# One transformer layer with product-key experts, fp32 split in two halves: order of the first expert table's products and place of the wait on its low half

## The chip, the cores and the metric

One core of a Trainium2 chip. The metric is the device time of one execution in microseconds (us). Before the change three runs took 958.69, 960.25 and 960.53 us, median 960.25.

## What is computed

One decoder layer on 256 tokens of width 1024: RMS norm, one input projection, eight heads of softmax attention and eight of stick-breaking attention, an output projection, then a feed-forward part of 16384 single-neuron experts chosen by product keys, then a gated per-layer embedding. The change is in the experts. The reference, cut to them:

```
# x: (256, 1024) normalised; u_table, v_table: (16384, 1024)
e_idx, gates = ...            # per token 8 heads x 16 experts, by two top-16 searches and a softmax
u = u_table[idx_c]
hid = gelu(einsum('cd,ced->ce', x_c, u))
out = einsum('ce,ced->cd', g_c * hid, v_table[idx_c])
```

The kernel does not gather. It multiplies all tokens with all 16384 rows of `u_table`, applies GELU, multiplies by a dense matrix of gates (zero for experts that were not chosen), and multiplies that with all of `v_table`.

## The kernel before

**Precision.** Every large product is made of three. A float32 operand is split into a high half (ACT casts it to the TensorE format `fp32r`) and a low half (the operand minus its high half, again `fp32r`), and hi x hi, hi x lo and lo x hi are summed in PSUM. The helper `three` (L1233) issues them in this order, piece by piece of the contraction.

**The first table's stage.** `u_table` comes as 128 tables `u_chunks[n]` of 128 experts: a tile of 128 x 1024 floats, 512 KB. One table is one *step* (numbered 0 to 127 here). The ring has four places (`RING`), q = n mod 4:

- SP loads table n into `t_raw[:, q]` once step n - 4 is done (`hid_done`, L361 to L364). After the last table the same ring goes on with `v_chunks` (L365 to L367).
- ACT makes `t_hi[:, q]` (`table_hi`, L597 to L599; semaphore `t_hi_ready`), two tables ahead of the GELU that it does between them (`LEAD` = 2).
- POOL makes `t_lo[:, q]` in the place of `t_raw` (`table_lo`, L1206 to L1209; semaphore `t_lo_pool`), after `t_hi_ready`.
- PE makes the step's 24 products (`hidden`, L1487 to L1490): eight pieces c of the contraction, for each `t_hi` x `xt_hi`, `t_hi` x `xt_lo`, `t_lo` x `xt_hi`, 128 x 128 weights with 256 columns (tokens), all into one PSUM bank. They are recorded under the helper's lines: L1236, L1237, L1238. The last one increments `hid_done`.
- ACT takes the bank through GELU, into `slots` for the first 40 tables (`FIRST`), in place for the later ones; there DVE multiplies it into `slots` (`late_gelu`, L1089).

**What PE waits for.** `u_lo(q, i)` (L271) is the semaphore `t_lo_pool` and the number of the table, and PE waits for it at the head of each step. There are three places: the first four steps (L1492 to L1498), the loop `u_steps` for steps 4 to 35 and again 36 to 39 (L1503 to L1508; the picks are transposed in between, L1510 to L1520), and `late_step` for steps 40 to 127 (L1530 to L1542). Each has one more wait at the head, for the PSUM bank or, in the first three, for the key scores (`s_out`, `gelu_done` or `late_used`). A late step has its 24 products followed, in three of four steps, by two waits and the four matmuls of `gates` (L1523 to L1528), until 64 sets are done. The order on every engine is the order written; the loops of all engines meet only through semaphores.

```
def u_lo(q, i):
    return t_lo_pool, RING * i + q + 1
```

**After the stage** PE takes the second table (`expert_sum`, L1553, lines L1565, L1567, L1568, 512 columns each), with the low halves made by DVE (L943), and then the gated embedding.

Of the kernel before, what the change touches and what calls it, by code (L numbers as in the profile page):

```python
# [27 lines left out]
P = 128  # L28
SEQ = 256
D = 1024  # L30
DC = D // P
# [13 lines left out]
RING = 4  # L45
LEAD = 2
FIRST = 40
# [24 lines left out]
def layer_program(nc, x, x_t, p_t, rel_bias, bucket_onehot, consts, qk_gain, w_in, w_out, w_query,  # L72
# [5 lines left out]
    with ctx:  # L78
# [11 lines left out]
        def tile(name, shape, offset, dt=f32):  # L90
            return nc.alloc_sbuf_tensor_at(name, shape, dt, offset=offset)

        h = tile("h", [P, TT, D], where["h"])
        xt_hi = tile("xt_hi", [P, DC, SEQ], where["xt_hi"], f32r)
        xt_lo = tile("xt_lo", [P, DC, SEQ], where["xt_lo"], f32r)
# [69 lines left out]
        t_lo = tile("t_lo", [P, RING, D], ZONE, f32r)  # L165
# [5 lines left out]
        t_hi = tile("t_hi", [P, RING, D], ZONE + 4 * 7168, f32r)  # L171
# [18 lines left out]
        def xt_half(k, c):  # L190
            return half(c // 2 + (4 if k == 2 else 0), c % 2)
# [4 lines left out]
        def hid_bank(q):  # L196
            return bank[(4, 5, 6, 5)[q % RING]][:, 0:SEQ]
# [12 lines left out]
        def sem(name):  # L210
            return ctx.enter_context(nc.semaphore(name))
# [36 lines left out]
        t_hi_ready, t_lo_ready, t_lo_pool = sem("t_hi_ready"), sem("t_lo_ready"), sem("t_lo_pool")  # L248
        lanes_ready, ones_ready, late_used = sem("lanes_ready"), sem("ones_ready"), sem("late_used")
        table_row = sem("table_row")  # L250
        hid_done, gelu_done = sem("hid_done"), sem("gelu_done")
# [19 lines left out]
        def u_lo(q, i):  # L271
            return t_lo_pool, RING * i + q + 1
# [120 lines left out]
        def _(act):  # L393
# [23 lines left out]
            def root(k, first, last):  # L417
                _, ms, rstd = norm_stats(k)
                nc.scalar.activation(rstd[:, first:last], ms[:, first:last], ACT.Sqrt).then_inc(root_ready, 1)
# [799 lines left out]
        def _(pe):  # L1219
            mm = nc.tensor.matmul  # L1220

            def transpose(src, tt, c, dst):
                return nc.tensor.transpose(dst, src[:, tt, P * c:P * (c + 1)], ident)
# [9 lines left out]
            def three(dst, pairs, last=None):  # L1233
                n = len(pairs)
                for c, ((ah, al), (bh, bl)) in enumerate(pairs):
                    mm(dst, ah, bh, start=(c == 0), stop=False)  # L1236
                    mm(dst, ah, bl, start=False, stop=False)  # L1237
                    ins = mm(dst, al, bh, start=False, stop=(c == n - 1))  # L1238
                return ins
# [40 lines left out]
            for c in range(DC):  # L1280
                pe.wait_ge(xt_lo_ready, c + 1)
                pe.wait_ge(quarter_lo, c + 1)
                for tt in range(TT):
                    t, dst = slice(P * tt, P * (tt + 1)), bank[4 + tt][:, :]
                    mm(dst, xt_hi[:, c, t], w_hi[:, 0, c, :], start=(c == 0), stop=False)
                    mm(dst, xt_hi[:, c, t], w_lo[:, 0, c, :], start=False, stop=False)
                    ins = mm(dst, xt_lo[:, c, t], w_hi[:, 0, c, :], start=False, stop=(c == DC - 1))
# [7 lines left out]
            for tt in range(TT):  # L1295
                ins = mm(bank[1][:, P * tt:P * (tt + 1)], neg_ones, diag[:, P * tt:P * (tt + 1)], start=True, stop=True)
# [8 lines left out]
            for g in range(8):  # L1305
                for tt in range(TT):
                    ins = nc.tensor.transpose(bank[g // 2][:, 256 * (g % 2) + P * tt:256 * (g % 2) + P * (tt + 1)],
                                              qk_nat[:, tt, 2 * g:2 * g + 2, :].rearrange("p a b -> p (a b)"), ident)
# [8 lines left out]
            for i in range(4):  # L1317
                if i >= 2:
                    pe.wait_ge(columns_out, 2 + i)
                for e in range(2):  # L1320
                    r = slice(HD * e, HD * (e + 1))
                    mm(bank[3 * e + i // 2][:, 256 * (i % 2):256 * (i % 2) + 256], qkt_s[r, 4 + i, 0:P], qkt_s[r, i, :],
                       start=(i % 2 == 0), stop=True, skip_group_check=True)
                for e in range(2):
                    r = slice(HD * e, HD * (e + 1))
                    ins = mm(bank[3 * e + 2][:, P * i:P * (i + 1)], qkt_s[r, 4 + i, P:SEQ], qkt_s[r, i, P:SEQ],
                             start=(i == 0), stop=True, skip_group_check=True)
# [42 lines left out]
            for hh in range(NH):  # L1370
                if hh % 4 == 0:
                    pe.wait_ge(s_exp, 1 + hh // 4)
                ins = nc.tensor.transpose(bank[hh // 4][:, P * (hh % 4):P * (hh % 4 + 1)], s0[:, hh, :], ident)
# [5 lines left out]
            for tt in range(TT):  # L1379
                for hh in range(NH):  # L1380
                    e, i = hh % 2, hh // 2
                    cols = slice(512 + HD * hh, 512 + HD * (hh + 1))
                    dst = bank[6 + tt][:, HD * hh:HD * (hh + 1)]
                    c = 256 * i + P * tt
                    ins = mm(dst, sb_w[:, e, c:c + P], v_all[:, 0, cols], start=True, stop=(tt == 0))
                    if tt:
                        ins = mm(dst, sb_w[:, e, 1024 + P * i:1024 + P * (i + 1)], v_all[:, 1, cols], start=False,
                                 stop=True)
# [3 lines left out]
            for hh in range(NH):  # L1392
                ins = mm(bank[0][:, HD * hh:HD * (hh + 1)], probs_t[:, hh // 4, P * (hh % 4):P * (hh % 4 + 1)],
                         v_all[:, 0, HD * hh:HD * (hh + 1)], start=True, stop=True)
# [3 lines left out]
            for hh in range(NH):  # L1398
                if hh % 4 == 0:
                    pe.wait_ge(s_exp, 3 + hh // 4)  # L1400
                for ss in range(2):
                    c = 256 * (hh % 2) + P * ss
                    ins = nc.tensor.transpose(bank[2 + hh // 2][:, c:c + P], s1[:, hh, P * ss:P * (ss + 1)], ident)
# [10 lines left out]
            for hh in range(NH):  # L1414
# [5 lines left out]
                for ss in range(2):  # L1420
                    c = 256 * (hh % 2) + P * ss
                    ins = mm(bank[1][:, HD * hh:HD * (hh + 1)], probs_t[:, place, c:c + P],
                             v_all[:, ss, HD * hh:HD * (hh + 1)], start=(ss == 0), stop=(ss == 1))
# [31 lines left out]
            for tt in range(TT):  # L1455
                pe.wait_ge(xs_ready, tt + 1)
                for c in range(DC):
                    ins = transpose(xs, tt, c, xt_half(2, c)[:, P * tt:P * (tt + 1)])
# [25 lines left out]
                    key_scores(n - 1)  # L1484
            key_scores(3)

            def hidden(q):  # L1487
                three(hid_bank(q), [((t_hi[:, q, P * c:P * (c + 1)], t_lo[:, q, P * c:P * (c + 1)]),
                                               (xt_hi[:, c, :], xt_lo[:, c, :])) for c in range(DC)]
                      ).then_inc(hid_done, 1)  # L1490

            for q in range(RING):  # L1492
                pe.wait_ge(*u_lo(q, 0))
                if q == RING - 1:
                    pe.wait_ge(gelu_done, q - 1)
                else:
                    pe.wait_ge(s_out, q + 1)
                hidden(q)  # L1498

            def bank_before(q):  # L1500
                return 2 if q % 2 else RING

            def u_steps(first, last):  # L1503
                with pe.Fori(first // RING, last // RING) as i:
                    for q in range(RING):
                        pe.wait_ge(*u_lo(q, i))
                        pe.wait_ge(gelu_done, RING * i + q - bank_before(q) + 1)
                        hidden(q)  # L1508

            u_steps(RING, PICKS_AT)  # L1510
            pe.wait_ge(hit_used, 2 * TT)
            for q in range(2):
                for tt in range(TT):
                    ins = nc.tensor.transpose(bank[q][:, P * tt:P * (tt + 1)], pick[:, tt, q, :], ident)
                ins.then_inc(pick_t_done, 1)
            pe.wait_ge(picks_ready, 1)
            for tt in range(TT):
                ins = nc.tensor.transpose(bank[2][:, P * tt:P * (tt + 1)],
                                          gate[:, tt, :, :].rearrange("p a b -> p (a b)"), ident)
            ins.then_inc(pick_t_done, 1)  # L1520
            u_steps(PICKS_AT, FIRST)

            def gates(k, s):  # L1523
                pe.wait_ge(hots_ready, s + 1)
                for q in range(4):
                    ins = mm(pairs[k][:, q, :, :].rearrange("p a b -> p (a b)"), hot_i[:, k, q, :],  # L1526
                             hot_j[:, k, q, :, :].rearrange("p a b -> p (a b)"), start=True, stop=True)
                ins.then_inc(gates_done, 1)  # L1528

            def late_step(q, j, first=False, last=False):  # L1530
                m, s = PAIR * j + q, 6 * j + 3 * (q // RING) + q % RING
                k = (3 * (q // RING) + q % RING) % 2
                pe.wait_ge(*u_lo(q, 2 * j + FIRST // RING))
                if first and q < bank_before(q):
                    pe.wait_ge(gelu_done, m + FIRST - bank_before(q) + 1)
                else:
                    pe.wait_ge(late_used, m - bank_before(q) + 1)
                hidden(q % RING)
                if q % RING < 3 and not (last and s >= SETS):
                    if not (first and s < 2):  # L1540
                        pe.wait_ge(gated, s - 1)
                    gates(k, s)  # L1542

            for q in range(PAIR):
                late_step(q, 0, first=True)
            with pe.Fori(1, N_PAIRS - 1) as j:
                for q in range(PAIR):
                    late_step(q, j)
            for q in range(PAIR):
                late_step(q, N_PAIRS - 1, last=True)  # L1550
# [39 lines left out]
            for q in range(RING - 2, RING):  # L1590
                ins = expert_sum(q, N_KEYS // RING - 1, tiles=(0,))
# [6 lines left out]
            for u, (tt, d0, width, b) in enumerate(END_PARTS):  # L1598
                t, d = slice(P * tt, P * (tt + 1)), slice(d0, d0 + width)
                dst = bank[b][:, 0:width]  # L1600
# [4 lines left out]
                for c in range(DC):  # L1605
                    if c % 2 == 0:
# [3 lines left out]
                    ins = mm(dst, xt_lo[:, c, t], wg_hi[:, c, d], start=False, stop=(c == DC - 1),  # L1610
                             skip_group_check=True)
# [66 lines left out]
```

## Time and profile before

| | |
|---|---|
| runs | 958.69, 960.25, 960.53 us |
| the profiled execution | 959.54 us, of which the span of the trace is 957.8 |
| granted clock of TensorE over the first table's stage | 1.00 of full speed |
| first table's stage, 188 to 580 us | PE busy 391.8 us, DVE 337.0, ACT 305.9, POOL 305.2 |
| loads of the first table | 128 of 512 KB, median 3.3 us from issue to landing |
| second table's stage | from 580.6 us on |

How to read it: PE is the matmul unit, PEld its weight loads, DVE the vector engine, ACT the scalar engine, POOL the GpSimd engine, SP the engine that issues the loads. A matmul is drawn longer than it holds the array, since matmuls overlap, so "busy" says that something is in flight; distances between starts tell the pace. L12 is line 12 of the kernel.

### The profile page before, as it was taken

Reading aid. Unit: us, or ns where it says so; the run is one execution under the profiler, and the core shown is the slowest. Engines: PE = TensorE matmul, PEld = TensorE weight load, DVE = VectorE, ACT = ScalarE, POOL = GpSimd, SP = SyncE. Lnnn points to the kernel's source line nnn. Section 1 sums busy time; section 2 is a strip of 40 time slices with the busy share of each in tenths; the row PEclk is TensorE's granted clock in tenths of the full one; section 3 lists DMA queues with packets and bytes.
Section 4 is the critical chain, followed back from the end, with each engine's and each line's share of the span. In section 5 each row is a group of like instructions: output and inputs, shape, how many; then the busy total and the mean of one; then the engine's idle time right before and its main releaser. Section 6 shows DMA issues by size and latency. Waiting matters only on the chain.

```text
span 957.8 us, 19183 instructions
## 1 busy us (share of the span) xinstructions
PE 948.6 (99%) x6222; PEld 863.8 (90%) x6222; DVE 686.2 (72%) x1391; ACT 614.4 (64%) x1037; POOL 329.9 (34%) x147
## 2 busy tenths in 40 slices
PE   8999999999999999999999999999999999999998
PEld 6887889999999999999999998788888888888887
DVE  6748863999975888888888874655555555566763
ACT  7568664456676888888888874555445445555643
POOL 0002310288888777777777772000000000000000
PEclk9999999999999999999999999999999999999999
DMA  9770363055565454444445455555566666555531
GB/s 332 272 289 1 113 255 133 2 178 192 179 189 183 158 175 157 171 157 172 164 165 168 160 176 181 193 193 185 193 238 242 236 230 234 197 196 188 191 105 44
DMA packets 46459, 172.08 MB, mean 180 GB/s; under 512 B 5043, under 2 KB 8540, under 8 KB 44892
## 3 DMA queue, kind: packets, MB, share of 16 engines
q1 hardware_dynamic: 46284, 171.40, 52.4%
q8 instruction: 19, 0.31, 0.1%
q10 hardware_dynamic: 144, 0.28, 0.1%
q14 instruction: 12, 0.10, 0.0%
HBM read 169.55 MB, written 2.11 MB: 179 GB/s over the span
## 4 chain that ended last, share of the span: by engine, by line
PE 89%; DVE 5%; DMA 3%; issue 2%; ACT 1%; POOL 1%; SPq 0%; DVEq 0%; POOLq 0%; ACTq 0%
PE bank L1237 12%; PE bank L1236 12%; PE bank L1238 12%; PE pair L1565 12%; PE pair L1567 12%; PE pair L1568 12%; PE pair L1526 3%; DMA w_raw<-w_in 2%; PE pair L1270 1%; PE pair L1272 1%; PE pair L1271 1%; PE bank L1610 1%; PE bank L1609 1%; PE bank L1252 1%; PE bank L1253 1%
## 5 line engine op out<-in xcount | busy, mean ns | idle before, releaser
L599 ACT ACTIVATE t_hi<-t_raw 128x1024 fp32r<-128x1024 f32 x256 | 270.5, 1057 | 187.3 <-DMA t_raw<-v_chunks 162.5
L1208 POOL TENSOR_TENSOR t_lo<-t_raw,t_hi 128x1024 fp32r<-128x1024 f32 x130 | 312.1, 2409 | 146.8 <-ACT t_hi L599 146.8
L1237 PE MATMUL bank<-xt_lo,t_hi 128*128 128x256 f32 x1024 | 287.4, 281 | 0.0
L1236 PE MATMUL bank<-xt_hi,t_hi 128*128 128x256 f32 x1024 | 287.2, 280 | 0.2 <-POOL t_lo L1208 0.2
L1238 PE MATMUL bank<-xt_hi,t_lo 128*128 128x256 f32 x1024 | 286.6, 280 | 0.0
L943 DVE TENSOR_TENSOR t_lo<-t_raw,t_hi 128x1024 fp32r<-128x1024 f32 x126 | 154.4, 1225 | 137.3 <-ACT t_hi L599 137.1
L1565 PE MATMUL pair<-t_hi,g_hi 128*128 128x512 f32 x512 | 199.6, 390 | 0.4 <-DVE g_lo L1123 0.4
L1567 PE MATMUL pair<-t_lo,g_hi 128*128 128x512 f32 x512 | 199.3, 389 | 0.0
L1568 PE MATMUL pair<-t_hi,g_lo 128*128 128x512 f32 x512 | 199.3, 389 | 0.0
L1236 PEld LDWEIGHTS bank<-xt_hi,t_hi 128*128 128x128 f32 x1024 | 192.8, 188 | 0.4 <-POOL t_lo L1208 0.4
L1238 PEld LDWEIGHTS bank<-xt_hi,t_lo 128*128 128x128 f32 x1024 | 193.1, 189 | 0.0
L1237 PEld LDWEIGHTS bank<-xt_lo,t_hi 128*128 128x128 f32 x1024 | 192.5, 188 | 0.0
L1565 PEld LDWEIGHTS pair<-t_hi,g_hi 128*128 128x128 f32 x512 | 96.1, 188 | 21.3 <-DVE g_lo L1123 1.3
L1567 PEld LDWEIGHTS pair<-t_lo,g_hi 128*128 128x128 f32 x512 | 96.1, 188 | 19.9
L1568 PEld LDWEIGHTS pair<-t_hi,g_lo 128*128 128x128 f32 x512 | 96.1, 188 | 19.7
L1076 DVE TENSOR_SCALAR hot_j<-bank,pick_t 128x128 fp32r<-128x128 f32 x256 | 86.9, 401 | 0.0
L650 ACT ACTIVATE hot_j<-hot_j,ratio 128x128 fp32r<-128x128 f32 x256 | 82.0, 394 | 0.0
L1092 DVE TENSOR_TENSOR slots<-slots,bank 128x256 f32 (+1 forms) x88 | 36.2, 412 | 31.4 <-ACT bank L663 31.4
L663 ACT ACTIVATE bank<-bank 128x256 f32<-128x256 f32 x88 | 32.4, 368 | 39.3 <-PE bank L1238 32.4
L1123 DVE TENSOR_TENSOR g_lo<-slots,g_hi 128x256 fp32r<-128x256 f32 x128 | 53.7, 420 | 0.6 <-ACT g_hi L673 0.6
L673 ACT ACTIVATE g_hi<-slots 128x256 fp32r (+1 forms) x128 | 51.2, 400 | 0.6 <-DVE slots L1092 0.6
L1086 DVE TENSOR_TENSOR slots<-slots,pair 128x512 f32 (+1 forms) x64 | 44.0, 687 | 7.5
(281 smaller groups left out, 1283.2 us busy)
## 6 DMA issues: line engine op xcount, KB each, us to landing
t_raw<-u_chunks SPq DMA_DIRECT2D x128, 512.0 KB, 3.3
t_raw<-v_chunks SPq DMA_DIRECT2D x128, 512.0 KB, 3.2
w_raw<-w_query SPq DMA_DIRECT2D x4, 2048.0 KB, 8.0
w_raw<-w_in SPq DMA_DIRECT2D x3, 2048.0 KB, 10.6
w_raw<-w_out SPq DMA_DIRECT2D x2, 2048.0 KB, 8.4
wg_raw<-w_gate SPq DMA_DIRECT2D x8, 512.0 KB, 4.8
w_raw<-w_in SPq DMA_DIRECT2D x7, 512.0 KB, 9.4
w_raw<-w_in SPq DMA_DIRECT2D x2, 1024.0 KB, 10.5
```

The costliest lines, as they stand in the source:

```text
L599: nc.scalar.activation(t_hi[:, q % RING, :], t_raw[:, q % RING, :], ACT.Copy).then_inc(t_hi_ready, 1)
L650: ins = nc.scalar.activation(hot_j[:, k, q, 1, :], hot_j[:, k, q, 0, :].bitcast(f32), ACT.Copy, scale=ratio[:, bass.ds(4 * s + q, 1)])
L943: nc.vector.tensor_tensor(t_lo[:, q % RING, :], t_raw[:, q % RING, :], t_hi[:, q % RING, :].bitcast(f32), ALU.subtract).then_inc(t_lo_read ...
L1076: nc.vector.tensor_scalar(hot_j[:, k, q, 0, :], lanes, pick_t[:, 1, bass.ds(t, 1)], pick_t[:, 2, bass.ds(t, 1)], ALU.is_equal, ALU.mult).t ...
L1123: nc.vector.tensor_tensor(g_lo[:, k, :], src, g_hi[:, k, :].bitcast(f32), ALU.subtract).then_inc(g_lo_ready, 1)
L1208: nc.gpsimd.tensor_tensor(t_lo[:, q, :], t_raw[:, q, :], t_hi[:, q, :].bitcast(f32), ALU.subtract).then_inc(t_lo_pool, 1)
L1236: mm(dst, ah, bh, start=(c == 0), stop=False)
L1237: mm(dst, ah, bl, start=False, stop=False)
L1238: ins = mm(dst, al, bh, start=False, stop=(c == n - 1))
L1565: mm(dst, g_hi[:, q, t], t_hi[:, q, d], start=first and q == 0, stop=False, skip_group_check=True)
L1567: mm(dst, g_hi[:, q, t], t_lo[:, q, d], start=False, stop=False, skip_group_check=True)
L1568: ins = mm(dst, g_lo[:, q, t], t_hi[:, q, d], start=False, stop=True, skip_group_check=True)
```

## The change

Of the 24 products of a step, the sixteen with the high half of the table are issued first, for all eight pieces, and then the eight with the low half. At the head of a step PE waits for `t_hi_ready` of that table instead of `t_lo_pool`; the wait for `t_lo_pool` stands between the sixteenth and the seventeenth product. All three places are changed in the same way. The other waits, the other engines and the other stages stay.

```diff
--- before.py
+++ after.py
@@ -1484,18 +1484,24 @@
                     key_scores(n - 1)
             key_scores(3)
 
-            def hidden(q):
-                three(hid_bank(q), [((t_hi[:, q, P * c:P * (c + 1)], t_lo[:, q, P * c:P * (c + 1)]),
-                                               (xt_hi[:, c, :], xt_lo[:, c, :])) for c in range(DC)]
-                      ).then_inc(hid_done, 1)
+            def hidden(q, lo_ready):
+                dst = hid_bank(q)
+                for c in range(DC):
+                    t = slice(P * c, P * (c + 1))
+                    mm(dst, t_hi[:, q, t], xt_hi[:, c, :], start=(c == 0), stop=False)
+                    mm(dst, t_hi[:, q, t], xt_lo[:, c, :], start=False, stop=False)
+                pe.wait_ge(*lo_ready)
+                for c in range(DC):
+                    ins = mm(dst, t_lo[:, q, P * c:P * (c + 1)], xt_hi[:, c, :], start=False, stop=(c == DC - 1))
+                ins.then_inc(hid_done, 1)
 
             for q in range(RING):
-                pe.wait_ge(*u_lo(q, 0))
+                pe.wait_ge(t_hi_ready, q + 1)
                 if q == RING - 1:
                     pe.wait_ge(gelu_done, q - 1)
                 else:
                     pe.wait_ge(s_out, q + 1)
-                hidden(q)
+                hidden(q, u_lo(q, 0))
 
             def bank_before(q):
                 return 2 if q % 2 else RING
@@ -1503,9 +1509,9 @@
             def u_steps(first, last):
                 with pe.Fori(first // RING, last // RING) as i:
                     for q in range(RING):
-                        pe.wait_ge(*u_lo(q, i))
+                        pe.wait_ge(t_hi_ready, RING * i + q + 1)
                         pe.wait_ge(gelu_done, RING * i + q - bank_before(q) + 1)
-                        hidden(q)
+                        hidden(q, u_lo(q, i))
 
             u_steps(RING, PICKS_AT)
             pe.wait_ge(hit_used, 2 * TT)
@@ -1530,12 +1536,12 @@
             def late_step(q, j, first=False, last=False):
                 m, s = PAIR * j + q, 6 * j + 3 * (q // RING) + q % RING
                 k = (3 * (q // RING) + q % RING) % 2
-                pe.wait_ge(*u_lo(q, 2 * j + FIRST // RING))
+                pe.wait_ge(t_hi_ready, RING * (2 * j + FIRST // RING) + q + 1)
                 if first and q < bank_before(q):
                     pe.wait_ge(gelu_done, m + FIRST - bank_before(q) + 1)
                 else:
                     pe.wait_ge(late_used, m - bank_before(q) + 1)
-                hidden(q % RING)
+                hidden(q % RING, u_lo(q, 2 * j + FIRST // RING))
                 if q % RING < 3 and not (last and s >= SETS):
                     if not (first and s < 2):
                         pe.wait_ge(gated, s - 1)
```

## Rows read from the trace of the kernel before

**Rows 1.** The page: span, engines, the chain that ended last.
```profile
span 957.8 us, 19183 instructions
...
PE 948.6 (99%) x6222; PEld 863.8 (90%) x6222; DVE 686.2 (72%) x1391; ACT 614.4 (64%) x1037; POOL 329.9 (34%) x147
...
PE 89%; DVE 5%; DMA 3%; issue 2%; ACT 1%; POOL 1%; SPq 0%; DVEq 0%; POOLq 0%; ACTq 0%
```

**Rows 2.** PE's waits: who waited for whom, us in total, times, longest.
```profile
PE pair L1565 <- DVE g_lo L1123: 0.4, 1, 0.4
...
PE bank L1236 <- POOL t_lo L1208: 0.2, 1, 0.2
```

**Rows 3.** Costliest groups: count | busy us, mean ns | idle before.
```profile
L1208 POOL TENSOR_TENSOR t_lo<-t_raw,t_hi 128x1024 fp32r<-128x1024 f32 x130 | 312.1, 2409 | 146.8 <-ACT t_hi L599 146.8
L1237 PE MATMUL bank<-xt_lo,t_hi 128*128 128x256 f32 x1024 | 287.4, 281 | 0.0
L1236 PE MATMUL bank<-xt_hi,t_hi 128*128 128x256 f32 x1024 | 287.2, 280 | 0.2 <-POOL t_lo L1208 0.2
L1238 PE MATMUL bank<-xt_hi,t_lo 128*128 128x256 f32 x1024 | 286.6, 280 | 0.0
```

**Rows 4.** Timeline around the head of step 2: start us, length us, instruction.
```profile
190.59 1.06 ACT L599 ACTIVATE t_hi<-t_raw 128x1024 fp32r<-128x1024 f32 x1
...
191.73 2.40 POOL L1208 TENSOR_TENSOR t_lo<-t_raw,t_hi 128x1024 fp32r<-128x1024 f32 x1 [11.69 <-ACT t_hi L599]
...
193.74 0.28 PE L1238 MATMUL bank<-xt_hi,t_lo 128*128 128x256 f32 x1
...
194.19 0.39 PE L1236 MATMUL bank<-xt_hi,t_hi 128*128 128x256 f32 x1 [0.17 <-POOL t_lo L1208]
...
194.41 0.28 PE L1237 MATMUL bank<-xt_lo,t_hi 128*128 128x256 f32 x1
```

**Rows 5.** Timeline around the head of step 24.
```profile
252.67 1.06 ACT L599 ACTIVATE t_hi<-t_raw 128x1024 fp32r<-128x1024 f32 x1 [0.19 <-DMA t_raw<-u_chunks]
...
253.80 2.49 POOL L1208 TENSOR_TENSOR t_lo<-t_raw,t_hi 128x1024 fp32r<-128x1024 f32 x1 [0.39 <-ACT t_hi L599]
...
256.34 0.28 PE L1238 MATMUL bank<-xt_hi,t_lo 128*128 128x256 f32 x1
256.46 0.35 PE L1236 MATMUL bank<-xt_hi,t_hi 128*128 128x256 f32 x1
256.64 0.28 PE L1237 MATMUL bank<-xt_lo,t_hi 128*128 128x256 f32 x1
```

**Rows 6.** Timeline: heads of steps 4, 19, 71, 72 and 80, gates and POOL before 72.
```profile
199.95 0.28 PE L1236 MATMUL bank<-xt_hi,t_hi 128*128 128x256 f32 x1
...
242.34 0.28 PE L1236 MATMUL bank<-xt_hi,t_hi 128*128 128x256 f32 x1
...
400.58 0.63 PE L1526 MATMUL pair<-hot_j,hot_i 128*128 128x256 f32 x4
...
400.73 2.41 POOL L1208 TENSOR_TENSOR t_lo<-t_raw,t_hi 128x1024 fp32r<-128x1024 f32 x1 [0.88 <-ACT t_hi L599]
...
401.05 0.28 PE L1236 MATMUL bank<-xt_hi,t_hi 128*128 128x256 f32 x1
...
403.86 0.28 PE L1236 MATMUL bank<-xt_hi,t_hi 128*128 128x256 f32 x1
...
429.25 0.28 PE L1236 MATMUL bank<-xt_hi,t_hi 128*128 128x256 f32 x1
```

**Rows 7.** Timeline of the query projection: every second to fourth column block's first product.
```profile
144.50 0.28 PE L1270 MATMUL pair<-xt_hi,w_hi 128*128 128x256 f32 x1
...
155.81 0.28 PE L1270 MATMUL pair<-xt_hi,w_hi 128*128 128x256 f32 x1
...
176.22 0.28 PE L1270 MATMUL pair<-xt_hi,w_hi 128*128 128x256 f32 x1
...
181.82 0.28 PE L1270 MATMUL pair<-xt_hi,w_hi 128*128 128x256 f32 x1
```

## The prediction

> **What bounds the kernel now.** I read the page first. TensorE is busy 948.6 us of a span of 957.8 us, and the chain that ended last is 89% PE [rows 1]. So the question is only how much the change gives to, or takes from, the uninterrupted row of matmuls. The changed lines run in the stage of the first expert table. It goes from the first product of step 0 at about 188 us to the last one of step 127 at about 580 us: 128 steps of 24 products, and between them 64 sets of four gate matmuls and six transposes.
>
> Second view: PE's waits [rows 2]. The wait on `t_lo`, which the change moves behind sixteen products, is listed once, with 0.2 us. Nothing else in this stage is listed.
>
> That view can hide small losses, because a matmul is drawn 280 ns long [rows 3] while the next one starts about 117 ns later. So I went by start times. A step of 24 products takes 2.82 to 2.83 us from start to start: fifteen steps from 199.95 to 242.34 give 42.39 / 15 = 2.826 us, 117.7 ns a product [rows 6]. I compared each start in the stage with the one before. A loss shows at step 2, and in smaller size at steps 20, 24 and 28 (each the head of a loop iteration); at all other step heads the interval is the usual 0.11 to 0.12 us, apart from the resumption after the transposes (step 36) and the first step, which the change leaves as they are.
>
> **Step 2** [rows 4]. POOL begins `t_lo` of table 2 at 191.73 and takes 2.40 us, until 194.13. The last product of step 1 starts at 193.74, the first of step 2 at 194.19: 0.45 us where 0.12 is usual. The next one follows after 0.22 instead of 0.12, a restart from an empty queue. Together 0.33 + 0.10 = 0.43 us. `t_hi` of the table was ready at 190.59 + 1.06 = 191.65, over 2 us before.
>
> **Step 24** [rows 5]. `t_lo` is ready at 253.80 + 2.49 = 256.29, the step starts at 256.46 on time, but its second product comes 0.18 us later, 0.06 more than usual. So the table was released just 0.17 us ahead and PE's queue was almost empty. This pattern stands three times in all; I put 0.2 us for the three together. The other steps of the early loop have a similar, thin lead of POOL (its 2.4 us [rows 3] against a step of 2.8), but lose nothing. `t_hi` was ready at 252.67 + 1.06 = 253.73, a lead of 2.7 us. In the loop of the late steps POOL leads by more: 400.73 + 2.41 = 403.14 against a start at 403.86 [rows 6].
>
> **The change, part by part.**
> Removed from the head of each step: the wait on `t_lo`, replaced by one on `t_hi`. It gives back what step 2 and the three thin steps lose: -0.43 - 0.2 = -0.6 us. All later work of PE moves with it, since the stage is uninterrupted, and the loads move too because they are released by the ends of steps. After step 2 the stall is gone and nothing is late next: with the head free, step 2 starts at about 193.86 and comes to its low products sixteen products later, 16 x 0.1177 = 1.88 us, at 195.74, when `t_lo` has been ready since 194.13. In the steady steps the lead at the new wait is 0.17 + 1.88 = 2.05 us at the least.
>
> Moved: the eight low products go behind the sixteen high ones. The count of matmuls and of weight loads stays, and the mean lengths of the three kinds are 280, 281 and 280 ns [rows 3]. One kind at 1 ns more or less over 1024 products is 1.0 us, so the new order is bounded to -1.0 and +1.0 us; I take zero, as the rows of the three kinds agree. The last product of a step still releases the bank for ACT and the buffer for the next load; it comes at the same place, 24 products after the first. Neither SP, ACT, DVE nor POOL gets or loses an instruction, and no DMA is moved past anything.
>
> Added: one wait on PE in each of 128 steps, between product 16 and 17. Queued behind it are the eight low products, the gates of the late steps, and behind their end ACT's GELU and SP's next load. It is met 2 us ahead, so its cost is only that of handing over one more instruction. The trace does not show that alone; the nearest rows do. Lower bound: at the step head of 256.34 to 256.46 [rows 5] two waits lie inside an interval of 0.12 us, and between 400.58 and 401.05 [rows 6] four gate matmuls and two waits take 0.47 us, 4 x 117.5 ns. So a satisfied wait costs nothing there. Upper bound: query columns without waits inside run 48 products in 181.82 - 176.22 = 5.60 us, 2.80 a 24 [rows 7]; the steps run at 2.826. If the two waits of a step made all of the 0.026 us, one is 13 ns, and 128 are 1.7 us. Against that reading, other query columns, also without waits, run at (155.81 - 144.50) / 4 = 2.83 us a 24 [rows 7]. And waits are denser in the late loop already: eight steps there hold 216 matmuls (192 and six sets of four) and 28 waits, 0.130 a matmul, in 429.25 - 403.86 = 25.39 us, 117.5 ns each [rows 6]; the early loop will have 12 waits to 96 products, 0.125. I take zero, and keep 1.7 us for the range.
>
> One rule speaks against the change. The trace has the waits at step heads inside a normal interval of 0.12 us [rows 5]. The Trainium skill (Advanced Engine Details and Errata, Network/Comms) gives 50 to 100 ns for a sequencer's reading of a semaphore value; if that stood on PE's path the change would cost 6 to 13 us. By that rule the heads with two waits would be 0.1 to 0.2 us longer than they are, so the trace does not agree that it lies on the path.
>
> **Sum.** -0.43 (step 2) - 0.2 (three thin steps) + 0 (order) + 0 (waits) = -0.6 us. The profiled execution took 959.54 us (span 957.8), so it would become 958.9; the median of the three runs is 960.25, 0.7 above it, and I predict against the median: 959.6 us. That is 0.06%, and a measurement of this kernel can tell from no change only about 0.2%, 1.9 us.
>
> **The rivals.**
> *Waits cost issue time.* At 13 ns each, -0.6 + 1.7 = +1.1 us: 961.3 (0.11%, still no measurable change). For it: the steps with waits are slower than some columns without. Against it: the slow columns without waits, and the late loop. Chance 0.12; it passes 0.2% only from 20 ns a wait ((1.9 + 0.6) / 128), and I give 0.02 to that.
> *The inner wait empties PE's queue (slower).* Place: between product 16 and 17 of all 128 steps. Mechanism: PE cannot prepare weights past a wait, so each step resumes from empty. Price: the resumption of step 2, 0.22 - 0.12 = 0.10 us [rows 4]; 128 x 0.10 = 12.8, less 0.6, gives 972.4 us. It decides once the wait is met less than about 0.17 us ahead (step 24's lead), or if a wait in the middle of a group behaves otherwise than one at its head. Against it: the 2 us of lead. The Trainium skill (TensorE: Matmul & The Clock Gate, spec table) has a 64-deep queue that pulls weight loads ahead of matmuls, and no row here shows whether a wait inside it stops that. Chance 0.07.
> *The products themselves run faster.* With the release 2 us ahead instead of 0.2, PE's queue is never shallow; if that is why a step takes 2.826 and not 2.80, all steps gain: 115 x 0.026 = 3.0 us, 956.6 us in all (0.37% faster). Against it: the late steps have a lead of 0.7 us and run no faster [rows 6]. Chance 0.09.
> *The change does nothing.* Step 2 could be held by something else once `t_lo` isn't, and stay where it is: 960.25. `s_out` for it was long there, so 0.05.
>
> **How the numbers follow.** Forecast 0.67 (0.02 of it seen as faster through scatter), nothing 0.05, issue time 0.12, faster products 0.09, emptied queue 0.07. Faster: 0.09 + 0.02 = 0.11. Slower: 0.07 + 0.02 = 0.09. Within 0.2%: 0.80. The forecast, the null and the issue-time case give 959.6 to 961.3; with the 1.0 us of the order and the scatter of the runs shown (958.69 to 960.53) the range is 957.7 to 961.7, and leaves out the two far cases.
>
> **What would show it.** In the changed profile: the wait on `t_lo` gone from PE's list; step 2 starting 0.12 us after step 1's last product; no 0.18 us interval at steps 24 and 28; eight starts of the low product in a row at the same 117 ns, with no longer interval before the first of them. The stage from step 0 to the first product of the second table should be shorter by 0.6 us. I am wrong if an interval of 0.15 us or more stands before the low products (emptied queue), if steps take 2.84 us (issue time), or if they take 2.80 (faster products).

## The result and the profile after

The changed kernel takes 962.92 us in the median of nine runs (962.43 to 971.27), the kernel before 958.88 (958.13 to 960.53): ratio 1.0045, 95% interval 1.0028 to 1.0061, so 4.0 us slower. I had forecast no measurable change, with 959.6 us and a range up to 961.7.

The page of the changed kernel. The profiled execution was the longest of the nine, 971.27 us, because of a stretch at a lower granted clock (the fifth of the 40 slices, 97 to 121 us), which ends before the first table's stage begins.

```profile
span 969.6 us, 19183 instructions
...
PE 961.3 (99%) x6222; PEld 876.9 (90%) x6222; DVE 694.0 (72%) x1391; ACT 613.0 (63%) x1037; POOL 329.1 (34%) x147
...
PEclk9999799999999999999999999999999999999999
...
PE 91%; DVE 5%; DMA 3%; ACT 1%; issue 0%; SPq 0%; DVEq 0%; ACTq 0%
```

PE bounds it as before [rows 1]. Its waits, the whole list:

```profile
PE bank L1279 <- DVE warm L765: 1.5, 1, 1.5
PE pair L1373 <- DVE s L850: 1.3, 1, 1.3
PE bank L1270 <- DVE w_lo L740: 0.6, 1, 0.6
PE bank L1223 <- ACT xs L557: 0.6, 1, 0.6
PE bank L1285 <- DVE w_lo L773: 0.2, 1, 0.2
PE pair L1571 <- DVE g_lo L1123: 0.2, 1, 0.2
```

The wait on `t_lo` [rows 2] is gone, and no new one stands in its place. Nothing waits longer, and yet the stage is longer. A second profile of the same kernel (962.10 us) shows where. Its timeline: the end of step 1 and the head of step 2, then the heads of steps 4 and 19.

```profile
191.95 0.28 PE L1492 MATMUL bank<-xt_lo,t_hi 128*128 128x256 f32 x1
192.07 1.12 PE L1495 MATMUL bank<-xt_hi,t_lo 128*128 128x256 f32 x8
193.03 0.28 PE L1491 MATMUL bank<-xt_hi,t_hi 128*128 128x256 f32 x1
...
198.73 0.28 PE L1491 MATMUL bank<-xt_hi,t_hi 128*128 128x256 f32 x1
...
241.53 0.28 PE L1491 MATMUL bank<-xt_hi,t_hi 128*128 128x256 f32 x1
```

The low row follows the last high product after 0.12 us, so the inner wait holds nothing back. The 0.45 us before step 2 [rows 4] are gone as well: its head comes 0.96 us after the low row began, 120 ns a product. But fifteen steps take 42.80 us, 2.853 each, where it was 2.826 [rows 6]. Over all 128 steps no interval between two starts, but for the restarts at steps 0 and 36, is longer than 124 ns. The products are simply further apart, all of them. The stage, from the first product of step 0 to the first of the second table, takes 583.91 - 187.25 = 396.66 us against 392.47 before, 4.2 more, which is the whole difference. The stages behind it are no longer than before.

The groups of the first profile after show it faintly, in the gates most clearly (L1532, L1526 before), whose code did not change:

```profile
L1491 PE MATMUL bank<-xt_hi,t_hi 128*128 128x256 f32 x1024 | 248.4, 281 | 0.0
L1492 PE MATMUL bank<-xt_lo,t_hi 128*128 128x256 f32 x1024 | 248.2, 281 | 0.0
L1495 PE MATMUL bank<-xt_hi,t_lo 128*128 128x256 f32 x1024 | 143.3, 283 | 0.0
L1532 PE MATMUL pair<-hot_j,hot_i 128*128 128x256 f32 x256 | 41.2, 283 | 0.0
L1532 PEld LDWEIGHTS pair<-hot_j,hot_i 128*128 128x128 f32 x256 | 35.3, 192 | 0.0
```

The same two groups of the kernel before:

```profile
L1526 PE MATMUL pair<-hot_j,hot_i 128*128 128x256 f32 x256 | 40.6, 280 | 0.0
L1526 PEld LDWEIGHTS pair<-hot_j,hot_i 128*128 128x128 f32 x256 | 34.5, 188 | 0.0
```

Gates and low row now have 283 ns and weight loads of 191 to 192 ns, where 280 and 188 to 189 ns stood. (The busy time of L1495 is smaller only because its eight matmuls overlap each other.) Averaged over the stage and without the restarts, the starts of the high products lie 118.4 to 118.8 ns apart, those of the low row 119.5, those of the gates 120.0. Before, those of the step's products lay 117.3 to 117.8 ns apart and those of the gates 117.9.

### The profile page after: what moved, and what is told of

Read it like the earlier page. It is cut to its first block, busy times and chain, and to the rows that moved or that the text cites. A ratio compares the mean times of both kernels' runs of the same rounds, so it can differ in the third digit from the quotient of the medians.

```text
span 969.6 us, 19183 instructions
## 1 busy us (share of the span) xinstructions
PE 961.3 (99%) x6222; PEld 876.9 (90%) x6222; DVE 694.0 (72%) x1391; ACT 613.0 (63%) x1037; POOL 329.1 (34%) x147
## 4 chain that ended last, share of the span: by engine, by line
PE 91%; DVE 5%; DMA 3%; ACT 1%; issue 0%; SPq 0%; DVEq 0%; ACTq 0%
PE bank L1495 13%; PE bank L1492 13%; PE bank L1491 12%; PE pair L1571 12%; PE pair L1573 12%; PE pair L1574 12%; PE pair L1532 3%; DMA w_raw<-w_in 2%; PE pair L1272 2%; PE pair L1270 2%; PE pair L1271 2%; PE bank L1615 1%; PE bank L1616 1%; PE bank L1253 1%; PE bank L1252 1%; PE bank L1251 1%
## 5 line engine op out<-in xcount | busy, mean ns | idle before, releaser
L1491 PE MATMUL bank<-xt_hi,t_hi 128*128 128x256 f32 x1024 | 248.4, 281 | 0.0
L1492 PE MATMUL bank<-xt_lo,t_hi 128*128 128x256 f32 x1024 | 248.2, 281 | 0.0
L1495 PE MATMUL bank<-xt_hi,t_lo 128*128 128x256 f32 x1024 | 143.3, 283 | 0.0
L1495 PEld LDWEIGHTS bank<-xt_hi,t_lo 128*128 128x128 f32 x1024 | 131.4, 191 | 0.0
```

Of the source, the lines that this page charges most:

```text
L1491: mm(dst, t_hi[:, q, t], xt_hi[:, c, :], start=(c == 0), stop=False)
L1492: mm(dst, t_hi[:, q, t], xt_lo[:, c, :], start=False, stop=False)
L1495: ins = mm(dst, t_lo[:, q, P * c:P * (c + 1)], xt_hi[:, c, :], start=False, stop=(c == DC - 1))
```

## The experiments

The diffs below are cut to the lines that matter. Two measures are used. The time is the median, with its ratio to the kernel before from the same chip (it is not simply the quotient of the two medians). The pace comes from the profile: a *step* is the mean of steps 4 to 18, from head to head (24 products), and *late eight* is the distance from the head of step 48 to that of step 56 (216 matmuls). Before, they are 2.827 and 25.39 us; in the changed kernel 2.853 and 25.71. One product at 120.0 ns makes 2.880 and 25.92.

**Wait or order?** Two kernels take one half of the change each, and a third goes further in its direction.

`order_only`: order of the changed kernel, but the wait on `t_lo` at the head and none inside (the diff is against the changed kernel).

```diff
-                pe.wait_ge(*lo_ready)
...
-                pe.wait_ge(t_hi_ready, q + 1)
+                pe.wait_ge(*u_lo(q, 0))
```

> The order of the changed kernel (sixteen high products, then eight low ones) with the wait on the low half at the head of the step, as before, and none in the middle. If the order costs the time: 962 to 964 us against 959 before (ratio about 1.004), the stage of the first table 396 to 397 us and a step 2.85 us. If the added wait in the middle costs it: 959 us (ratio 1.000), the stage 392 to 393 us, a step 2.82 to 2.83 us.

`wait_only`: order and head of the kernel before, and a satisfied wait inside (`extra` is the `t_hi_ready` of this table once more).

```diff
                     mm(dst, t_hi[:, q, t], xt_hi[:, c, :], start=(c == 0), stop=False)
+                    if c == 5:
+                        pe.wait_ge(*extra)
                     mm(dst, t_hi[:, q, t], xt_lo[:, c, :], start=False, stop=False)
```

> The order of the kernel before (hi hi, hi lo, lo hi for each piece), the wait on the low half at the head, and one more wait, on the high half, which is long met, between product 16 and 17. If an inner wait costs the time (about 30 ns in each of 128 steps): 962 to 964 us, a step 2.85 us. If the order costs it: 959 us, a step 2.82 to 2.83 us.

`three_sweeps`: the wait at the head, and three rows of eight products, so that no two neighbours share their weights.

```diff
+                order = [(hi(c), xt_hi[:, c, :]) for c in range(DC)]
+                order += [(hi(c), xt_lo[:, c, :]) for c in range(DC)]
+                order += [(lo(c), xt_hi[:, c, :]) for c in range(DC)]
```

> Wait at the head; order: eight high x high, eight high x low, eight low x high, so that no two neighbours share weights and every sweep repeats one kind. If what costs is a long row of products of one kind with new weights each time (119.6 ns in the changed kernel's low row against 118.6 in its high pairs): 24 x 119.6 = 2.87 us a step, about 961 to 965 us. If neighbours with the same weights matter for nothing and the interleaving of before is no better than any other: 959 us.

`after_again` is the changed kernel, for the second profile shown above.

> The changed kernel once more, for a second profile. Both theories: 962 to 964 us, the stage of the first table 396 to 397 us from its first product to the second table's first, a step 2.85 us; if the profile recorded first (971.27 us, with a stretch of lower granted clock ahead of the stage) was odd in the stage too, another value.

Measured: `order_only` 962.80 us, ratio 1.0046 (1.0033 to 1.0060), step 2.853, late eight 25.71, all as in the changed kernel. `wait_only` 958.51 us, ratio 0.9995 (0.9986 to 1.0004), step 2.827, late eight 25.39, all as before. `three_sweeps` 965.21 us, 1.0063 (1.0050 to 1.0077), 2.867 and 25.81. `after_again` 962.10 us. The timelines, heads of steps 4 and 19 of `wait_only`:

```profile
199.72 0.28 PE L1491 MATMUL bank<-xt_hi,t_hi 128*128 128x256 f32 x1
...
242.12 0.28 PE L1491 MATMUL bank<-xt_hi,t_hi 128*128 128x256 f32 x1
```

and of `order_only`, with the head of its step 2 ahead:

```profile
193.26 0.38 PE L1494 MATMUL bank<-xt_hi,t_hi 128*128 128x256 f32 x1
...
199.07 0.28 PE L1494 MATMUL bank<-xt_hi,t_hi 128*128 128x256 f32 x1
...
241.87 0.28 PE L1494 MATMUL bank<-xt_hi,t_hi 128*128 128x256 f32 x1
```

42.40 and 42.80 us for the fifteen steps. So the order costs the time and the wait costs nothing. The two kernels also price what the late wait gives: the stage of `order_only` is 397.06 us, that of the changed kernel 396.67, and the 0.39 us between them are the stall at step 2. The going further in `three_sweeps` costs more: its stage is 398.71 us.

**What about the order?** Four more orders.

`blocks_of_two`: high products of two pieces, then their two low ones.

```diff
+                for c in range(0, DC, 2):
+                    order += [(hi(k), x[:, k, :]) for k in (c, c + 1) for x in (xt_hi, xt_lo)]
+                    order += [(lo(k), xt_hi[:, k, :]) for k in (c, c + 1)]
```

> Four high products (two pieces), then the two low ones of these pieces, four times; wait at the head. If each pair of neighbours has its own price (118.0 within a piece, 118.6 from pair to pair, 119.6 from low to low, 117.9 from low to high): 118.3 ns a product, 2.84 us a step, 961 us (ratio 1.002). If only long rows of one kind settle at a slow pace: 2.82 to 2.83 us a step, 959 us (ratio 1.000).

`low_shuffled`: the low row in another order of pieces.

```diff
+                order += [(lo(c), xt_hi[:, c, :]) for c in (0, 5, 2, 7, 4, 1, 6, 3)]
```

> The order of the changed kernel with the wait at the head, but the eight low products take the pieces as 0 5 2 7 4 1 6 3, so that addresses no longer go up by one piece each time. If the regular step of the addresses makes the low row slow: its products fall from 119.6 to about 118 ns, a step 2.84 us, 961.5 us (ratio 1.003). If it is the row of one kind, whatever the addresses: 119.6 ns stays, 2.85 us, 962.8 us (ratio 1.0045).

`low_second`: threes with the low product in the middle, wait at the head.

```diff
+                    order += [(hi(c), xt_hi[:, c, :]), (lo(c), xt_hi[:, c, :]), (hi(c), xt_lo[:, c, :])]
```

> In threes as before, but high x high, low x high, high x low, so that no two neighbours inside a piece share weights; this is the order of the query projection, whose columns run at 2.80 or 2.83 us. If sharing weights with the neighbour were what makes the order of before fast: slower, 2.85 us a step and 962 us. If threes are fast in any order: 2.80 to 2.83 us a step, 956 to 959 us (ratio 0.996 to 1.000).

`lagged`: threes, the low product of piece c - 2 after the high ones of piece c, and the wait on `t_lo` ahead of the first low one.

```diff
+                    if c == 2:
+                        pe.wait_ge(*lo_ready)
+                    if c >= 2:
+                        ins = mm(dst, t_lo[:, q, P * (c - 2):P * (c - 1)], xt_hi[:, c - 2, :], start=False, stop=(c == DC + 1))
```

> The low products again between the high ones in threes, but two pieces late, with the wait on the low half after six products and the wait on the high half at the head. If what costs is a row of eight low products (119.6 ns each) and of high pairs without a low one between them (118.5), this order has neither: a step 2.82 to 2.83 us, 958.4 to 959 us (ratio 0.999 to 1.000), and the 0.45 us before step 2 shrinks to 0.12. If any order that is not exactly that of before costs (a price of each pair of neighbours): the three kinds of neighbours are those of before but for the piece of the low one, so 959 too; if the address of the low product's piece matters: 2.84 to 2.86 us a step and 961 to 963 us.

| kernel | median us | ratio (95%) | step | late eight |
|---|---|---|---|---|
| blocks_of_two | 963.48 | 1.0036 (1.0016 to 1.0056) | 2.853 | 25.71 |
| low_shuffled | 964.08 | 1.0064 (1.0034 to 1.0095) | 2.853 | 25.71 |
| low_second | 958.60 | 1.0007 (0.9976 to 1.0038) | 2.800 | 25.39 |
| lagged | 959.51 | 1.0010 (0.9984 to 1.0036) | 2.830 | 25.49 |

Length of the rows is not it: a row of two low products costs as much as one of eight. Which piece is read is not it either. Threes are fast, also when the low product comes from another piece. Sharing the weights with the neighbour is not it: in `low_second` no two neighbours inside a piece share them, and it is as fast as the order of before. Its 2.800 is no gain of the order, though. Its late eight is that of the kernel before, its stage 391.69 us against 392.47, and its ratio can't be told from 1. `blocks_of_two` went against both expectations: a price for each pair of neighbours would have made it 2.84, and slowness of long rows alone 2.82 to 2.83.

**One order has two paces.** The kernel before has the 2.800 too. Steps 37, 38 and 39 come after the restart at step 36, with the same order, addresses and waits as steps 4 to 18; heads of steps 37 and 40:

```profile
293.92 0.28 PE L1236 MATMUL bank<-xt_hi,t_hi 128*128 128x256 f32 x1
...
302.32 0.28 PE L1236 MATMUL bank<-xt_hi,t_hi 128*128 128x256 f32 x1
```

8.40 us for three steps is 2.800 each. In `low_second` it is the other way round: 2.800 in steps 4 to 18 and 2.827 in steps 37 to 39. The query projection, whose code and addresses are the same in both kernels, shows it as well. Four of its column blocks took 11.31 us in the kernel before [rows 7], 2.827 a 24; in the second profile of the changed kernel the same four take 11.20 us, 2.800:

```profile
143.78 0.28 PE L1270 MATMUL pair<-xt_hi,w_hi 128*128 128x256 f32 x1
...
154.98 0.28 PE L1270 MATMUL pair<-xt_hi,w_hi 128*128 128x256 f32 x1
```

In the first profile of the changed kernel they take 11.31 us again. So order and addresses do not fix the pace of threes: they run at 2.800 or at 2.827, and the changes seen come after restarts. The slow orders show one pace each: the changed kernel, `order_only`, `low_shuffled` and `blocks_of_two` come back to 2.853 after step 36, and `three_sweeps` to 2.867.

**Where do the operands lie?** A low row reads only `xt_hi` as moving operand; the threes mix in `xt_lo`. From the kernel's list of tiles, `xt_lo` starts 8192 + 128 bytes after `xt_hi`, since the 128 bytes of `gains` lie between, while the pieces are 1024 bytes apart and the tables start a multiple of 256 bytes from `xt_hi`. So `xt_lo` is the one operand that lies elsewhere within a 256-byte line. My expectations spoke of 512-byte lines; that was the wrong size, as will be seen. `pads` below are unused bytes.

`xt_lo_aligned` (on the changed kernel) and `before_xt_lo_aligned`:

```diff
-        sizes = dict(h=2 * D, xt_hi=DC * SEQ, gains=4 * DC, xt_lo=DC * SEQ, cst=4 * P, qkg=32, stats=192)
+        sizes = dict(h=2 * D, xt_hi=DC * SEQ, pad_a=96, gains=4 * DC, xt_lo=DC * SEQ, cst=4 * P, qkg=32, stats=192, pad_b=32)
```

> The changed kernel with xt_lo moved up by 384 bytes and the tables by 512, so that all four operands lie at the same distance (128 bytes) from a 512-byte line; before, xt_lo was the only one that did not. If the place of xt_lo is what makes the high pairs faster (118.6 ns) than the low row (120): the pairs go to 120 ns, a step to 2.88 us, 966 us (ratio 1.008). If not: 2.853 us and 962.8 us.

> The kernel before with the same move of xt_lo by 384 bytes and of the tables by 512. If the place of xt_lo is what keeps its order at 117.5 to 117.8 ns a product: 120 ns, a step 2.88 us, 966 us (ratio 1.008), and the order of the products then matters for nothing. If the order alone is it: 2.82 us a step and 959 us.

`zone_256` (on the changed kernel) and `before_zone_256`: only `pad_b=64`, 256 bytes.

> The changed kernel, with all that lies behind the small tiles (the table halves t_lo and t_hi among it) 256 bytes further up in each partition, so that the weights no longer lie at the same distance from a 512-byte line as xt_hi. If the pace of a product depends on how the addresses of the weights and of the moving operand stand to each other: the 120 ns of the low row change (117 to 119, or more), a step leaves 2.853 us, and the time 962.8 us. If only the order of the kinds sets the pace: low row 120 ns, a step 2.853 us, 962.8 us (ratio 1.0045).

> The kernel before with the tables 256 bytes further up. If relative addresses matter: a step other than 2.8265 us in the early loop, by up to 0.05 us to either side. If only the order of the kinds: 2.8265 us early, 117.5 ns a product late, 959 us (ratio 1.000).

| kernel | median us | ratio (95%) | step | late eight |
|---|---|---|---|---|
| xt_lo_aligned | 967.43 | 1.0081 (1.0057 to 1.0105) | 2.880 | 25.92 |
| before_xt_lo_aligned | 967.59 | 1.0088 (1.0061 to 1.0115) | 2.880 | 25.92 |
| zone_256 | 962.78 | 1.0041 (1.0025 to 1.0057) | 2.853 | 25.71 |
| before_zone_256 | 958.87 | 0.9991 (0.9977 to 1.0006) | 2.829 | 25.39 |

With `xt_lo` moved, every product of the stage takes 120.0 ns, in both orders, and the order has no effect any more (stages of 400.09 and 400.43 us; the stall at step 2 is the 0.35 us between them). The kernel before with `xt_lo` moved, heads of steps 4 and 19:

```profile
201.29 0.28 PE L1236 MATMUL bank<-xt_hi,t_hi 128*128 128x256 f32 x1
...
244.49 0.28 PE L1236 MATMUL bank<-xt_hi,t_hi 128*128 128x256 f32 x1
```

and its groups:

```profile
L1236 PE MATMUL bank<-xt_hi,t_hi 128*128 128x256 f32 x1024 | 290.1, 283 | 0.1
L1238 PE MATMUL bank<-xt_hi,t_lo 128*128 128x256 f32 x1024 | 289.8, 283 | 0.0
L1237 PE MATMUL bank<-xt_lo,t_hi 128*128 128x256 f32 x1024 | 289.8, 283 | 0.0
```

All three kinds now have the 283 ns of the low row. 43.20 us for fifteen steps is 2.880 each. 512 bytes of padding cost 8.9 us (967.59 against 958.69), twice what the change cost: 8.0 us in the stage, and most of the rest in the query projection, which multiplies the same two tiles and now takes 2.880 a 24 as well.

**Which property of the place?** Other distances of `xt_lo` in the kernel before (`pad_a` and `pad_b` of 128 and 384 bytes for 256; 256 and 256 for 384; 448 and 64 for 64), and, in the changed kernel, pieces of `xt_hi` that start 1088 bytes apart:

```diff
-        xt_hi = tile("xt_hi", [P, DC, SEQ], where["xt_hi"], f32r)
+        xt_hi = tile("xt_hi", [P, DC, SEQ + 16], where["xt_hi"], f32r)[:, :, 0:SEQ]
```

> The kernel before with xt_lo 256 bytes (within a 512-byte line) above xt_hi instead of 128. If only the equality of the two places is bad: 2.80 to 2.83 us a step and 958 to 959 us. If the size of the distance counts: another value, to either side, up to 2.88 us and 967 us.

> The same with 384 bytes, that is 128 below. If the direction counts as little as the size: 2.80 to 2.83 us a step. If the direction counts: other than with 128.

> The same with 64 bytes. If the size of the distance counts: between 2.83 and 2.88 us a step, 959 to 967 us. If only equality is bad: 2.80 to 2.83 us.

> The changed kernel with 64 bytes between the pieces of xt_hi (pieces 1088 bytes apart instead of 1024), so that the low row, which reads xt_hi alone, no longer starts each product at the same distance from a 512-byte line. If a product's pace hangs on how the start of its moving operand has moved, within such a line, against the one before it: the low row leaves 120 ns (116 to 119, or more than 120), a step is not 2.853 us. If it hangs on which of the two tiles is read: 120 ns in the low row, 2.853 us, 962.8 us.

| kernel | median us | ratio (95%) | step | late eight |
|---|---|---|---|---|
| before_delta_256 | 967.81 | 1.0079 (1.0052 to 1.0105) | 2.880 | 25.92 |
| before_delta_384 | 958.54 | 0.9984 (0.9963 to 1.0005) | 2.827 | 25.39 |
| before_delta_64 | 963.56 | 1.0037 (1.0017 to 1.0057) | 2.880 | 25.57 |
| after_stride_64 | 960.97 | 1.0025 (1.0004 to 1.0046) | 2.841 | 25.55 |

A distance of 256 is as bad as 0, and 384 gives the paces of 128 to the last digit. So, as far as these five distances go, what counts is the place within 256 bytes. 64 lies between in the late steps and is as bad as 0 in the early ones up to step 35; in steps 37 to 39, after the restart, it runs at 2.827. `after_stride_64` takes away about half of the loss of the changed kernel without touching its order, which ties that loss to the addresses.

**The weights, and the late wait in a good order.** `zone_256` and `before_zone_256` had moved the weights by 256 bytes, and their time and paces stayed. If the line is 256 bytes long they could show nothing about the weights' place; `before_zone_128` (`pad_b=32`) can. `lagged_low_second` has the order high x high of piece c, low x high of piece c - 2, high x low of piece c, with the late wait.

> The kernel before with the tables, and so the weights, 128 bytes further up; the distance between xt_hi and xt_lo stays 128. The earlier move by 256 bytes could not show anything if the line is 256 bytes long, as the runs with the moved xt_lo now suggest. If only the moving operands count: late steps 117.5 ns a product, early ones 2.80 to 2.84 us, 959 us (ratio 1.000). If the weights' place counts too: another pace, by 1 ns a product or more (3 us or more in the time).

> The late wait kept, in an order that alternates the moving tiles in threes: high x high of piece c, low x high of piece c - 2, high x low of piece c; wait on the low half after four or five products. If the rule of the moving operands' places holds, the steps take 2.80 to 2.83 us and the stall at step 2 is gone: 957.5 to 958.9 us (ratio 0.9985 to 1.000), clearly below the changed kernel. If a low product that lags behind costs by itself: 2.85 us a step and 962 us.

`before_zone_128`: 964.79 us, ratio 1.0084 (1.0051 to 1.0117), step 2.880, late eight 25.60. The heads of steps 4 and 19:

```profile
200.46 0.28 PE L1236 MATMUL bank<-xt_hi,t_hi 128*128 128x256 f32 x1
...
243.66 0.28 PE L1236 MATMUL bank<-xt_hi,t_hi 128*128 128x256 f32 x1
```

Its stage is 397.01 us against 392.47. So the weights' place counts too, and the 128 bytes between the moving tiles did not help the early steps here. The padding moves everything that lies behind it, also what ACT, POOL and the loads write; of the operands of a step's products it moves the weights alone. `lagged_low_second`: 959.14 us, ratio 0.9996 (0.9978 to 1.0013), step 2.818, late eight 25.47: no stall at step 2, and none of the loss of the changed kernel, but no gain either: its stage is 392.67 us against 392.47, as a slower late loop takes back what the stall gave. I had expected 957.5 to 958.9 us. No version was found that is measurably faster than the kernel before.

## Why the prediction was wrong

- **Bound and stage**: right. PE is the bound, the whole difference lies in the first table's stage, and the stages behind it keep their lengths.
- **The stall at step 2, -0.43 us**: right. It is gone; `order_only` against the changed kernel puts it at 0.39 us.
- **The three thin steps, -0.2 us**: mis-sized. `wait_only` has the order and the head waits of the kernel before and none of these intervals, and its stage is 392.43 us against 392.47. In the trace of before, the steps behind them ran at about 2.800 us (25, 26 and 27), so the longer intervals at 20, 24 and 28 cost nothing in sum: the term measures 0.04 us. They are absent from the changed kernel, as forecast, but give nothing back.
- **The added wait, 0 us**: right. `wait_only` is at 0.9995 (0.9986 to 1.0004) and its stage is 392.43 us against 392.47; at 13 ns a wait it would have been 1.7 us longer. The bound from above, a step with waits against a column without, compared two paces that had nothing to do with waits. The Trainium skill (Advanced Engine Details and Errata, Network/Comms) gives 50 to 100 ns for reading a semaphore value from a sequencer. If each met wait in PE's stream cost that, 128 of them would cost 6.4 us or more (an estimate from that page's figure); `wait_only` shows nothing of it.
- **The new order, 0 us within -1.0 and +1.0**: this step failed. "As the rows of the three kinds agree" was the reason given, and it does not hold: the three kinds agreed because they stood in that order. The order measures 397.06 - 392.47 = +4.59 us (`order_only`). Bounding a new order by the spread of the old one's groups bounds nothing, since the price of a product depends on the order in which it stands. The sum with the measured terms is 4.59 - 0.39 = +4.2 us; the stage shows 4.20 and the medians 4.04. The top of my range, 961.7 us, is also no sum of its parts (960.53 + 1.0 = 961.5, 961.3 + 1.0 = 962.3); the result lies above each of them.
- **Rivals**: the slower one, an emptied queue behind the inner wait, named another mechanism and 972.4 us. It is refuted: the interval ahead of the low row is 0.11 to 0.12 us in every step. The faster one asked the right question, why a step takes 2.826 and not 2.80 us, and blamed the queue. Its own row, query columns at 2.80 and at 2.83 without any wait, was the sign that a stream of the same instructions can have more than one pace, and I used it only to acquit the waits. So were the steps at 2.800 us in the stage itself (37 to 39), which have both waits at their head; my reading that a step takes 2.82 to 2.83 us passed over them.
- Of what I said would show it, "steps take 2.84 us" came nearest (2.853), and I had tied it to issue time.

The Trainium skill (TensorE: Matmul & The Clock Gate, Back-to-back issue gap) gives 262 cycles at 2.4 GHz for 256 columns, which is 109 ns, as the spacing of isolated matmuls, and says that in a stream with weight loads both instructions set it. The trace agrees that it is more here: 116.7 ns a product is the best step measured and 120.0 the worst, and in these runs it depends on order and addresses, and even then takes more than one value.

## What to carry to other kernels

When PE is the bound, an order of matmuls is not free to change even if every dependence allows it: compare distances between starts over whole periods before and after, at a resolution of 1 ns, since the list of waits showed nothing of this loss. If two operands are read in turn, look at where they and the weights start within 256 bytes, and measure: here 128 bytes between the two moving tiles save 8.9 us, by an accident of a small tile that lies between them, and 128 bytes more under the weights cost 5.7 (964.79 against 959.09). The slowest case met was the one with all of them at the same place.

## What the runs showed of the hardware that I had not expected

A product of 256 fp32r columns with its weight load has no fixed pace. When all weights and moving operands start at the same place within 256 bytes, each takes 120.0 ns from start to start, in both orders that were tried (2.880 us for 24). With `xt_lo` 128 bytes off it depends on the order: 2.853 for high pairs and a low row, and 2.800 or 2.827 for threes, of which the same code shows now one and now the other. It is not a sum over pairs of neighbours: `order_only` and `blocks_of_two` come out at the same 2.853.

The pace carries over. The four gate matmuls have the same code and addresses in all kernels of one layout, and take 117.9 ns each in the kernel before, behind threes, and 120.0 in the changed one, behind a low row. After a restart the low row of step 2 of `order_only` runs at 118.6 ns a product, that of the next step at 119.6. In most kernels steps settle at 2.800, 2.827, 2.853, 2.867 or 2.880 us, all of them multiples of 13.33 ns (210, 212, 214, 215 and 216 times), as if the period had to fit into something that repeats. Elsewhere it is a longer period that repeats: `after_stride_64` takes 2.829 and 2.851 us in turn, 5.680 together (426 times), and `lagged` 2.828 and 2.832. What that is, the runs do not show: a conflict between the two streams that PE reads would fit the dependence on both addresses, but this is argued and not shown. A conflict with what other engines and the loads read and write was not tested. Why threes settle lower than pairs with a low row, and what decides between their two paces, stays open too.
